# Prompt attention of a hybrid decoder step: 16 heads one by one, and by pairs

## What is computed

```python
def sparse_attend(q, ks, vs, valid):        # 16 heads of 64, 4 KV heads
    s = jnp.einsum('btgrd,btkgd->btgrk', qg, ks).astype(jnp.float32) * (HEAD_DIM ** -0.5)
    s = jnp.where(valid[:, :, None, None, :], s, -jnp.inf)
    p = jax.nn.softmax(s, axis=-1).astype(vs.dtype)
    o = jnp.einsum('btgrk,btkgd->btgrd', p, vs)
...
def dsa_prompt(q, k, v, iq, ik, iw):
        score = indexer_scores(iqb, ik, iwb)               # 8 indexer heads, relu, weighted sum
        score = jnp.where(allowed[None], score, -jnp.inf)
        _, idx = lax.top_k(score, topk)                    # the 128 best keys of each query
        valid = idx <= qpos[None, :, None]
        return sparse_attend(qb, _gather_rows(k, idx), _gather_rows(v, idx), valid)
```

## Time and profile before

| | us |
|---|---|
| median of 3 runs | 6118.93 (6109.17 to 6125.71) |
| the profiled execution | 6095.56 |
| its span, first to last instruction | 6093.8 |
| the eight attention stages together | 688.2 |
| layer 0, W = 128, 256, 384, 512 | 33.8, 68.1, 100.4, 121.2 |
| layer 1, W = 128, 256, 384, 512 | 50.7, 97.4, 98.7, 117.9 |

### The profile page before, as it was taken

One profiled execution on the slowest core, in us unless ns is written; L12 is line 12 of the kernel. 1 busy time (PEld: TensorE's weight loads), 2 busy tenths in 40 slices (PEclk: granted clock), 3 DMA queues, 4 the chain that ended last, 5 costly groups with the idle time before them and its releaser, 6 DMA issues. The chain is left out here.

```text
span 6093.8 us, 52161 instructions
## 1 busy us (share of the span) xinstructions
PE 4488.3 (74%) x16596; PEld 2712.1 (45%) x16596; DVE 3624.1 (59%) x8352; ACT 1143.9 (19%) x2862; POOL 2491.0 (41%) x2215
## 2 busy tenths in 40 slices
PE   6965982577878777469788777588777878547768
PEld 5344872453534555153444556273443566212223
DVE  4056437755656667676665767774566565854441
ACT  2022310111222111020222212111222201101111
POOL 0000010245433764436543444226433475377775
PEclk9965995788889988789898989799889989779999
DMA  3300740467565998679777976458666798599998
GB/s 128 112 17 19 260 146 0 158 232 258 180 213 183 381 336 302 205 269 373 264 234 247 390 271 227 130 181 306 206 205 202 266 394 315 187 351 409 395 377 306
DMA packets 574392, 1467.90 MB, mean 241 GB/s; under 512 B 59448, under 2 KB 250264, under 8 KB 567608
## 3 DMA queue, kind: packets, MB, share of 16 engines
q0 software_dynamic: 307200, 1115.82, 51.5%
q1 hardware_dynamic: 253960, 314.47, 15.3%
q10 hardware_dynamic: 12960, 34.26, 1.4%
HBM read 1418.60 MB, written 45.80 MB: 240 GB/s over the span
## 5 line engine op out<-in xcount | busy, mean ns | idle before, releaser
L2621 PE MATMUL bank<-vring,diag 128*128 128x512 f32 (+1 forms) x3064 | 1565.5, 649 | 474.7 <-ACT diag L2602 192.2
L2507 POOL DMA_INDIRECT uring<-in_peer_u,eidx x1024 | 1186.9, 1159 | 1227.3 <-DVE uring L2539 742.3
L2574 POOL DMA_INDIRECT vring<-in_peer_v,eidx x1024 | 1134.3, 1108 | 1336.7 <-PE bank L2621 935.1
L2539 DVE SCALAR_TENSOR_TENSOR uring<-uring,xr 128x1024 f32<-128x1024 f32 x1040 | 1263.9, 1222 | 585.2 <-DMA uring<-in_peer_u,eidx 540.0
L2621 PEld LDWEIGHTS bank<-vring,diag 128*128 128x128 f32 (+1 forms) x3064 | 572.8, 202 | 1279.7 <-issue 815.4
L634 PE MATMUL bank<-wt,xT 128*128 128x512 f32 (+3 forms) x1440 | 606.3, 580 | 90.1 <-DMA wt<-in_w_in 82.6
L2602 ACT ACTIVATE diag<-ident,wt 128x128 f32<-128x128 f32 x750 | 289.0, 398 | 1149.6 <-PE bank L2621 1034.1
L634 PEld LDWEIGHTS bank<-wt,xT 128*128 128x128 f32 (+1 forms) x1440 | 241.0, 178 | 444.1 <-issue 348.0
L2654 DVE SCALAR_TENSOR_TENSOR x_tok<-vring,wt,x_tok 128x1024 f32<-128x1024 f32 x274 | 356.7, 1302 | 90.8 <-DMA vring<-in_peer_v,eidx 76.8
L489 PE MATMUL bank<-xT,wx 128*128 128x264 f32 (+1 forms) x1536 | 371.6, 405 | 34.0 <-DMA wx<-in_w_in 33.8
L489 PEld LDWEIGHTS bank<-xT,wx 128*128 128x128 f32 x1536 | 307.7, 202 | 87.3 <-DMA wx<-in_w_in 34.1
(11 more groups left out here) (464 smaller groups left out, 5507.5 us busy)
## 6 DMA issues: line engine op xcount, KB each, us to landing
wt<-in_w_in SPq DMA_DIRECT2D x32, 2048.0 KB, 12.7
wx<-in_w_in SPq DMA_DIRECT2D x48, 1024.0 KB, 6.5
wm<-in_w_in SPq DMA_DIRECT2D x32, 1024.0 KB, 22.6
wm<-in_w_branch_a SPq DMA_DIRECT2D x32, 1024.0 KB, 15.4
wq<-in_peer_wq SPq DMA_DIRECT2D x32, 1024.0 KB, 9.0
tokm<-tout ACTq DMA_DIRECT2D x64, 256.0 KB, 4.6
s_h<-in_state_ssm SPq DMA_DIRECT2D x16, 1024.0 KB, 9.5
wm<-in_w_branch_b SPq DMA_DIRECT2D x16, 1024.0 KB, 13.4
```

The source lines that it names most:

```text
L2507: pool.indirect_dma_start(out=G.uring[:, K % UR, :], out_offset=None, in_=table, in_offset=bass.IndirectOffsetOnAxis(ap=E.tiles[q][3][:, j ...
L2539: dve.scalar_tensor_tensor(row, row, 1.0, G.xr[:, q % 2, :], ALU.mult, ALU.mult, accum_out=G.pre[:, q % 2, j:j + 1]).then_inc(G.dotted, 1)
L2574: pool.indirect_dma_start(out=G.vring[:, K % VR, :], out_offset=None, in_=table, in_offset=bass.IndirectOffsetOnAxis(ap=E.tiles[q][3][:, j ...
L2621: mm = pe.matmul(G.bank[6 + c][0:m, :], G.diag[:, R % DR, 0:m], G.vring[:, K % VR, c * BANK:(c + 1) * BANK], start=first, stop=last, skip_ ...
```

## The change

All heads of `attention_prompt` are taken by pairs. Banks are now halves of four two-bank tiles, `duo`. One VectorE instruction masks the scores of two heads (2W columns, the mask broadcast), one takes both maxima, and one negates them. `exp` stays one per head, since each has its own bias. One ScalarE copy moves the turned probabilities of two heads, and one relu covers two indexer heads. The scores of a pair go back to back into `duo[0]`, which is a single buffer (the next pair's scores wait for the mask of this pair); the turns go to `duo[1]`, also single. The values of all 16 heads stay in banks 4 and 5, and `attend_out` is gone: at the end there is one reciprocal and two scaled copies of 512 columns. On TensorE the order inside a pair is score(p+1), attend(p-1), turn(p), and expert work is put in at two places of a pair, before the scores and before the turns. Indexer dots use `duo[2]` and `duo[0]` in turn.

```diff
@@ -1075,20 +1075,24 @@
     with ExitStack() as mem, stage(nc, G, "attn", key) as (block, sem):
         def sb(name, shape):
             return mem.enter_context(nc.sbuf_tensor(name, shape, F32, allow_name_mangling=True))
-        rel = sb("rel", [P, 2, SEQ])
+        pT = sb("pT", [P, 2, 2, SEQ])
+        rel = pT
         sc = sb("score", [P, SEQ])
         bias = sb("bias", [P, SEQ])
         iw = sb("iw", [P, IH])
         best = sb("best", [P, 8])
-        s = sb("s", [P, 2, SEQ])
-        pT = sb("pT", [P, 2, SEQ])
+        s = sb("s", [P, 2, 2, SEQ])
         mx, den, rden = sb("mx", [P, AH]), sb("den", [P, AH]), sb("rden", [P, AH])
         yb = sb("yb", [P, AW])
-        bank = G.bank
+        bank, duo = G.bank, G.duo
         KT = t + 1
         W = KT * P
+        NP2 = AH // 2
         f0 = 0.12
         f1 = 0.45 if W > TOPK_P else 0.15
+        def at(p):
+            return f1 + (0.95 - f1) * max(0.0, min(NP2, p)) / NP2
 
         @block.sync
         def _(sp):
@@ -1101,48 +1105,54 @@
         @block.tensor
         def _(pe):
             go = G.beside.by(pe, "PE")
-            for h in range(IH):
...
+            for i in range(IH // 2):
+                if i >= 2:
+                    pe.wait_ge(sem("relu"), i - 1)
+                go(f0 * i / (IH // 2))
+                for q in range(2):
+                    lo = q * IDIM
+                    mm = pe.matmul(duo[2 * ((i + 1) % 2)][:, q, 0:W], S.iqT[lo:lo + IDIM, i, :], G.ikT[lo:lo + IDIM, 0:W], start=True, stop=True)
+                mm.then_inc(sem("dots"), 1)
+            def score(p):
+                for q in range(2):
+                    h = 2 * p + q
+                    g = h // REP
+                    lo, c = (g % 2) * HD, (g // 2) * REP + h % REP
+                    mm = pe.matmul(duo[0][:, q, 0:W], S.qT[lo:lo + HD, c, :], G.kT[lo:lo + HD, g // 2, 0:W], start=True, stop=True)
+                mm.then_inc(sem("qk"), 1)
+            def turn(p):
+                pe.wait_ge(sem("exp"), 2 * p + 2)
+                if p >= 1:
+                    pe.wait_ge(sem("pT"), p)
+                for q in range(2):
+                    for c in range(KT):
+                        tr = pe.transpose(duo[1][:, q, c * P:(c + 1) * P], s[:, p % 2, q, c * P:(c + 1) * P], G.ident[:])
                 tr.then_inc(sem("pturned"), 1)
 
+            def attend(p):
+                pe.wait_ge(sem("pT"), p + 1)
+                for q in range(2):
+                    h = 2 * p + q
+                    for c in range(KT):
+                        mm = pe.matmul(bank[4 + h // 8][:, (h % 8) * HD:(h % 8 + 1) * HD], pT[:, p % 2, q, c * P:(c + 1) * P],
+                                       G.v[:, c, (h // REP) * HD:(h // REP + 1) * HD], start=(c == 0), stop=(c == KT - 1))
+                mm.then_inc(sem("pv"), 1)
+            pe.wait_ge(sem("relu"), IH // 2)
             score(0)
-            score(1)
...
+            for p in range(NP2):
+                go(at(p + 0.3))
+                if p + 1 < NP2:
+                    pe.wait_ge(sem("masked"), p + 1)
+                    score(p + 1)
+                if p >= 1:
+                    attend(p - 1)
+                go(at(p + 0.7))
+                turn(p)
+            attend(NP2 - 1)
+            go(0.96)
+            pe.wait_ge(sem("o"), 2)
             for k in range(KD):
                 tr = pe.transpose(bank[k // 4][:, (k % 4) * P:(k % 4 + 1) * P], yb[:, k * P:(k + 1) * P], G.ident[:])
                 if k % 4 == 3:
@@ -1151,27 +1161,24 @@
         @block.scalar
         def _(act):
             go = G.beside.by(act, "ACT")
-            for h in range(IH):
...
+            for i in range(IH // 2):
+                go(f0 * i / (IH // 2))
+                act.wait_ge(sem("dots"), i + 1)
+                if i >= 2:
+                    act.wait_ge(sem("summed"), 2 * (i - 1))
+                act.activation(rel[:, i % 2, :, 0:W], duo[2 * ((i + 1) % 2)][:, :, 0:W], ACT.Relu).then_inc(sem("relu"), 1)
+            for p in range(NP2):
+                go(at(p + 0.35))
+                act.wait_ge(sem("max"), p + 1)
+                for q in range(2):
+                    h = 2 * p + q
+                    act.activation(s[:, p % 2, q, 0:W], s[:, p % 2, q, 0:W], ACT.Exp, bias=mx[:, h:h + 1],
+                                   accum_out=den[:, h:h + 1]).then_inc(sem("exp"), 1)
+                go(at(p + 0.8))
+                act.wait_ge(sem("pturned"), p + 1)
+                if p >= 2:
+                    act.wait_ge(sem("pv"), p - 1)
+                act.activation(pT[:, p % 2, :, 0:W], duo[1][:, :, 0:W], ACT.Copy).then_inc(sem("pT"), 1)
 
         @block.vector
         def _(dve):
@@ -1181,11 +1188,12 @@
             sm = Own(dve, sem("summed"))
             for h in range(IH):
                 go(f0 * (h + 0.5) / IH)
-                dve.wait_ge(sem("relu"), h + 1)
+                dve.wait_ge(sem("relu"), h // 2 + 1)
+                r = rel[:, h // 2 % 2, h % 2, 0:W]
                 if h == 0:
-                    sm(dve.tensor_scalar(sc[:, 0:W], rel[:, 0, 0:W], iw[:, 0:1], None, ALU.mult))
+                    sm(dve.tensor_scalar(sc[:, 0:W], r, iw[:, 0:1], None, ALU.mult))
                 else:
-                    sm(dve.scalar_tensor_tensor(sc[:, 0:W], rel[:, h % 2, 0:W], iw[:, h:h + 1], sc[:, 0:W], ALU.mult, ALU.add))
+                    sm(dve.scalar_tensor_tensor(sc[:, 0:W], r, iw[:, h:h + 1], sc[:, 0:W], ALU.mult, ALU.add))
 
             seen, diag = slice(0, W), slice(W - P, W)
             top = Own(dve, sem("top"))
@@ -1201,33 +1209,30 @@
             else:
 
                 top(dve.tensor_copy(bias[:, seen], G.causal[:]))
-            for h in range(AH):
...
+            for p in range(NP2):
+                go(at(p))
+                dve.wait_ge(sem("qk"), p + 1)
+                if p >= 2:
+                    dve.wait_ge(sem("pturned"), p - 1)
+                sp2 = s[:, p % 2, :, seen]
+                dve.scalar_tensor_tensor(sp2, duo[0][:, :, seen], HD ** -0.5, bias[:, seen].unsqueeze(1).to_broadcast([P, 2, W]),
                                          ALU.mult, ALU.add).then_inc(sem("masked"), 1)
-                dve.wait_ge(sem("masked"), h + 1)
...
+                dve.wait_ge(sem("masked"), p + 1)
+                m = mx[:, 2 * p:2 * p + 2]
+                top(dve.tensor_reduce(m, sp2, AX.X, ALU.max))
+                dve.tensor_scalar(m, m, -1.0, None, ALU.mult).then_inc(sem("max"), 1)
             go(0.95)
-            for h in (AH - 2, AH - 1):
-                attend_out(dve, sem, top, yb, bank, den, rden, h)
+            dve.wait_ge(sem("exp"), AH)
+            top(dve.reciprocal(rden[:], den[:]))
+            dve.wait_ge(sem("pv"), NP2)
+            for q in range(2):
+                dve.tensor_tensor(yb[:, q * BANK:(q + 1) * BANK].rearrange("p (h d) -> p h d", d=HD),
+                                  bank[4 + q][:].rearrange("p (h d) -> p h d", d=HD),
+                                  rden[:, 8 * q:8 * q + 8].unsqueeze(2).to_broadcast([P, 8, HD]), ALU.mult).then_inc(sem("o"), 1)
             go(0.98)
             for q in range(2):
                 dve.wait_ge(sem("yturned"), q + 1)
                 dve.tensor_copy(G.ybT[:, 4 * q:4 * q + 4, j * P:(j + 1) * P], bank[q][:].rearrange("p (k c) -> p k c", c=P))
-
...
 
 
 
@@ -2697,7 +2702,8 @@
         def expert_sem(name, i):
             return top.enter_context(nc.semaphore(name, num=EXPERT_SEM0 + i))
         G.beside, G.stages, G.stale = Beside(), 0, []
-        G.bank = [top.enter_context(nc.psum_tensor(f"bank{i}", [P, BANK], F32)) for i in range(8)]
+        G.duo = [top.enter_context(nc.psum_tensor(f"duo{i}", [P, 2, BANK], F32)) for i in range(4)]
+        G.bank = [G.duo[i // 2][:, i % 2, :] for i in range(8)]
         G.x = sb("x_tok", [P, NT + 1, D])
         G.xT = sb("xT", [P, KD, 2 * P + DECB])
         G.ident, G.ones, G.triu = sb("ident", [P, P]), sb("ones", [P, 1]), sb("triu", [P, P])
```

More of the change, by code:

```diff
@@ L1103, in _ @@
             go = G.beside.by(pe, "PE")
-            for h in range(IH):
-                if h >= 2:
-                    pe.wait_ge(sem("relu"), h - 1)
-                lo = (h % 2) * IDIM
-                go(f0 * h / IH)
-                pe.matmul(bank[4 + h % 2][:, 0:W], S.iqT[lo:lo + IDIM, h // 2, :], G.ikT[lo:lo + IDIM, 0:W],
-                          start=True, stop=True).then_inc(sem("dots"), 1)
-            def score(h):
-                g = h // REP
-                lo, j = (g % 2) * HD, (g // 2) * REP + h % REP
-                if h >= 2:
-                    pe.wait_ge(sem("masked"), h - 1)
-                pe.matmul(bank[h % 2][:, 0:W], S.qT[lo:lo + HD, j, :], G.kT[lo:lo + HD, g // 2, 0:W],
-                          start=True, stop=True).then_inc(sem("qk"), 1)
@@ L1120, in turn @@
-            def turn(h):
-                pe.wait_ge(sem("exp"), h + 1)
-                if h >= 2:
-                    pe.wait_ge(sem("pT"), h - 1)
-                for c in range(KT):
```

(49 more changed lines are left out.)

10 lines of the change are left out of this document (removed).

## The result

The kernel after takes **6088.1 us** (median of 5 runs, 6084.1 to 6094.8) beside 6118.9 before: ratio 0.9949, 95% interval 0.9933 to 0.9965. Run twice more beside the kernel before, it stood at 0.9933 (0.9910 to 0.9956; 6034.5 against 6073.0 us) and 0.9933 (0.9914 to 0.9951; 6082.6 against 6125.9). The three medians lie 30.8, 38.5 and 43.2 us under those of before; 36.5 was forecast. (One of the six executions behind 6082.6 took 17955.7 us at a granted clock of 0.59 and is left out of the ratio.) The first two profiles, though, differ by only 11.4 us of span (6093.8 and 6082.4). That gap had to be explained first.

The account below looks back on a forecast made before the run. TensorE was taken to bound the heads phase, VectorE the top-k, each waiting for the other in the indexer. Terms -18.9 - 4 - 11.5 - 13.5 + 11.4 = -36.5 us, from 6118.9 to 6082 us; range 6056 to 6110.

Parts of the forecast that it names:

- a stage's gain is passed on whole: Eight attention stages, 688.2 us together: each ends for all engines, so gains pass on unless a transfer outlives the stage.
- ends of the terms: Low and high limits given for single terms of the sum; stated to give -13 to -65 us if they go together.
- Score visits: Heads phase: TensorE goes over to scores 8 times a stage instead of 15, 0.35 us each; 18.9 us gained.
- Eleventh slot: Ahead of the second pair's score, one more slot of expert work fills TensorE's idle time; six slots, 11.5 us gained.
- Start of the heads phase: After the top-k, TensorE's first work waits only for the pair's mask; 0.5 us a stage, 4 us gained.
- Indexer: Indexer phase by pairs of heads: 2.0 us less with slots, 1.2 to 1.5 without; 13.5 us gained together.
- End: End of a stage: both scaled copies come last and TensorE waits for the last pair's copy; 11.4 us lost.
- The rival with a rising clock: Layer 0's two stages without experts go to full clock in their heads phases; -30 us on top, about 6052; chance 0.08.
- The one with a falling clock: Over 100 us of six stages' heads phases run at half clock, costing 55 us; about 6140 us; chance 0.08.
- Lost: Visit overhead turns up elsewhere and the eleventh slots come late; only -6 to -17 us, 6102 to 6113; chance 0.26.

Follow-up runs that it names:

- end_early: The changed kernel with its end partly undone: first eight heads normalised behind pair 6's mask, their four final transposes ahead of the last attend; ratio 0.9905, windows 623.0 us.
- again_after: The changed kernel, nothing altered, run again beside the kernel before for a second profile; 6034.5 against 6073.0 us, ratio 0.9933.
- again_before: The kernel before, nothing altered, run again for a second profile of its last phase; ratio 1.0003.
- third_after: The changed kernel, nothing altered, run a third time beside the kernel before; 6082.6 against 6125.9 us, ratio 0.9933.
- before_cut: The kernel before without the experts of layer 1's second half (their sums missing in the output); 5321.7 us.
- idx_only: The kernel before with the indexer alone by pairs (relu of two heads at a time); ratio 0.9963, windows 657.0 us.
- after_cut: The changed kernel without the experts of layer 1's second half (their sums missing in the output); 5281.5 us.

## Why the prediction was right

- **The sum.** -36.5 us forecast; the windows gave -36.9 and -40.4 in the pairs of profiles from one chip and -55.0 in the first pair, the medians -30.8, -38.5 and -43.2. The assumption that a stage's gain is passed on whole held to within the 6 us above. That the medians (37.5 in the mean) come out so near to 36.5 is in part luck: the windows gave 43.3 in the mean, and 6.0 of them went again outside the stages for a reason that is not shown. The prediction's ends of the terms, as it states them, add up to -8 and -51 us (18.9 + 4 + 0 + 5 - 20 and 18.9 + 4 + 18 + 18 - 8), not to -13 and -65; the measured values lie inside either.
- **Score visits, -18.9.** Undone: 16.6. In steady state 0.34 a visit, forecast 0.35. In the stages of 128 and 256 columns the price was not the forecast one (above). By the Trainium skill ("TensorE: Matmul & The Clock Gate", Part 2) two exposed loads of 107 ns would be 0.21, an estimate; the trace has more. What else is exposed at a visit, and whether it hangs on the height of the weights, no run here shows.
- **Eleventh slot, -11.5.** Undone: 10.3. The sum agrees, the split does not: 11.5 was six slots at 1.92 us, and the runs have four that are worth 1.9 to 3.3 us each (in three of them more of the stage runs at half the clock without the slot in place, 17.2 us instead of 10.3 in the first of 384 columns), and two (128 and 256 columns of layer 1) that are worth nothing. The idle time is 5.8 us where I had put it under 5; 7.2 less the slot's 1.9 would be 5.3.
- **Start of the heads phase, -4.** Not tested by itself, so it stays an estimate. Beside it stands a wait that I had not seen: 1.1 us for the last relu ahead of score(0). At 512 columns it lies ahead of slots behind which TensorE is idle for 5.8 us anyway, and only shifts idle time there. In the stage of 128 columns of layer 1 it is 2.06 us and nothing covers it. The second pair's score was reckoned at the full clock; at half the clock it brought the first turn to 4.99 us behind the start of the mask (4672.34 and 4667.35) instead of 4.0.
- **Indexer, -13.5.** Alone: 15.1 and 19.8, and 13.5 without the clock at the end of the stages of 512 columns.
- **End, +11.4.** end_early took 12.5 back, but part of that (transposes in the copy's wait) before did not have either, so the term's size was not measured by itself. The waits were forecast at 1.3 and 1.5 us (1.11 and 1.45 measured).
- **What was not in the sum** is the clock. Before, the ends of the 512-column stages ran at 0.50 in five of six cases (for 6.9 us, which costs 3.2, or for half of that; after, about 1 us is left, the final transposes' 1.71 against 1.10 in the earlier trace rows), and the stage of 256 columns of layer 1 took 97.3, 91.4 and 91.5 us, after 82.1 to 83.7. With the first pair's 15.3 us in that stage, where the terms give about 6 (2.45 + 0.5 + 1.92 + 1.3, and 0 for the end), this is most of what lies between 55 and 36.5. The rival with a rising clock had looked at the two layer 0 stages at 0.50 throughout; these stayed there (0.50 and 0.53). The one with a falling clock had a small part: the fall in the stage of 128 columns of layer 1 costs 1.6 or 3.3 us in three of four profiles, far from the 55 it asked for. "Lost" found nothing: visits and slot were both paid back in the sum.

## What to carry to other kernels

Ask of a change by pairs not how many instructions go, but how often the bound engine changes over between kinds of work, and price that from the distance of two starts in steady state. An idle stretch ahead of a long serial phase is a place to put work, but the helper's instruction on the other engine has to move along, ahead of whatever waits there. And compare a change of half a per cent by stage windows of several profiles and by medians: a single pair of profiles said 11 us here for what is 37.

## What the runs showed of the hardware

- The same stream of expert rows ran at 403 to 409 GB/s in some profiles (before, again_after) and at 350 to 380 in others (after, again_before, third_after), of either kernel, and a program of 6100 us was 40 to 50 us longer with it.
- The same wait of 1.11 us of TensorE was followed by a granted clock of 0.50 in one profile (before_cut) and of 1.00 in another (idx_only); so was the same wait of 2.06 us in after_cut and after.
